# Two diffusion-backbone layers on one core: the order of the three token tiles in attention

## The reference

```python
for l in range(2):
    # prompt: attends to the prompt alone
    a_q, a_k, a_v, b_q, b_k, b_v = project_heads(xp * (1 + p_sc1) + p_sh1, w_in[l], qk_gain[l])
    mix_p = mixer_output(...)                    # 128 keys
    # sample: attends to its 256 keys and 128 cached ones
    a_q, ... = project_heads(xs * (1 + s_sc1) + s_sh1, w_in[l], qk_gain[l])   # and axial rotary
    a_k = concatenate([a_k, cache_a_k[:, l]], axis=1)                         # likewise a_v, b_k, b_v
    mix_s = mixer_output(...)                    # 384 keys
    # mixer_output: 4 differential heads, softmax(q1 k1) - lam * softmax(q2 k2), times v, RMS-normed,
    #               8 GQA query heads over 2 kv heads, both concatenated and times w_out[l]
    # then x = LayerNorm(alpha * x + gate * mix), a dense SwiGLU (layer 0) or top-2-of-8 experts (layer 1)
```

## Time and profile before

| | us |
|---|---|
| median of 3 runs | 1724.61 (1721.42 to 1729.32) |
| the profiled execution, its own time | 1731.87 |
| span of its profile | 1730.0 |
| attention of layer 0: first scores to the transposes of o | 142.77 to 235.66 |
| attention of layer 1, the same | 681.37 to 774.51 |

### The profile page before, as it was taken

The page is one execution under the profiler, slowest core; times in us unless marked ns, Lnnn a source line. Parts: engine busy times, 40 slices in busy tenths (PEclk is TensorE's granted clock), DMA queues, the critical chain, the costliest instruction groups (busy, mean ns, idle before and its releaser), DMA issues. The chain is left out here.

```text
span 1730.0 us, 24774 instructions
## 1 busy us (share of the span) xinstructions
PE 1554.8 (90%) x9179; PEld 1036.2 (60%) x9180; DVE 752.9 (44%) x1215; ACT 575.3 (33%) x979; POOL 90.6 (5%) x109
## 2 busy tenths in 40 slices
PE   4798989999999899988898999989999799999891
PEld 1684577788887486466623565645556477677430
DVE  0473776333333654675501443434344443233215
ACT  0433545223331442450202333433343433233101
POOL 2010012200000010000100000000000000000002
PEclk8899999999999899999699999999999999999896
DMA  9244536933441644532999999999999378787992
GB/s 344 98 146 161 195 122 208 342 122 113 146 146 50 219 138 137 192 133 74 401 364 376 385 389 393 386 343 378 375 393 376 126 292 292 276 294 264 359 352 101
DMA packets 206705, 432.49 MB, mean 250 GB/s; under 512 B 11896, under 2 KB 52856, under 8 KB 206304
## 3 DMA queue, kind: packets, MB, share of 16 engines
q1 hardware_dynamic: 195712, 390.64, 62.3%
q0 software_dynamic: 7712, 29.05, 4.6%
q10 hardware_dynamic: 3136, 10.88, 1.9%
HBM read 409.55 MB, written 20.97 MB: 249 GB/s over the span
## 5 line engine op out<-in xcount | busy, mean ns | idle before, releaser
L2004 PE MATMUL ps<-d_ring_parts,scratch_parts 128*128 128x512 f32 (+1 forms) x444 | 172.1, 388 | 13.9 <-DVE hT_parts L1318 9.1
L1825 DVE TENSOR_TENSOR cst<-cst,ps 128x256 f32<-128x256 f32 (+2 forms) x89 | 32.7, 368 | 241.5 <-ACT cst L1156 241.5
L2405 PE MATMUL ps<-ring,hT 128*32 128x256 f32 x1760 | 119.9, 389 | 10.3 <-DMA ring<-in_w_moe_up 9.2
L2004 PE MATMUL ps<-gu_ring_parts,scratch_parts 128*128 128x512 f32 (+1 forms) x336 | 128.7, 383 | 0.0
L2399 PE MATMUL ps<-ring,hT 128*64 128x512 f32 (+1 forms) x512 | 113.1, 584 | 15.9 <-issue 8.5
L2004 PE MATMUL ps<-d_ring_parts,hT_parts 128*128 128x512 f32 (+1 forms) x312 | 119.0, 382 | 0.0
L1181 ACT ACTIVATE qkv_parts<-ring 128x1024 fp32r<-128x1024 f32 x102 | 103.1, 1050 | 13.2 <-issue 13.0
L2004 PEld LDWEIGHTS ps<-d_ring_parts,scratch_parts 128*128 128x128 f32 x444 | 84.7, 191 | 32.2 <-issue 9.3
L2004 PE MATMUL ps<-gu_ring_parts,o_parts 128*128 128x512 f32 x264 | 104.0, 394 | 0.0
L2405 PEld LDWEIGHTS ps<-ring,hT 128*32 128x32 f32 x1760 | 55.9, 111 | 61.2 <-issue 15.7
L1164 ACT ACTIVATE cst<-ps 128x128 f32<-128x128 f32 (+1 forms) x51 | 16.0, 315 | 224.9 <-PE ps L2421 215.5
(11 more groups left out here) (385 smaller groups left out, 3150.1 us busy)
## 6 DMA issues: line engine op xcount, KB each, us to landing
ring<-in_w_moe_gate SPq DMA_DIRECT2D x176, 512.0 KB, 9.7
ring<-in_w_moe_up SPq DMA_DIRECT2D x176, 512.0 KB, 11.1
ring<-in_w_moe_down SPq DMA_DIRECT2D x176, 512.0 KB, 9.6
gu_ring<-in_w_ada SPq DMA_DIRECT2D x48, 1024.0 KB, 7.4
gu_ring<-in_w_in SPq DMA_DIRECT2D x16, 1024.0 KB, 7.4
gu_ring<-in_w_ffn_gate SPq DMA_DIRECT2D x11, 1024.0 KB, 5.5
gu_ring<-in_w_ffn_up SPq DMA_DIRECT2D x11, 1024.0 KB, 8.1
d_ring<-in_w_ffn_down SPq DMA_DIRECT2D x11, 1024.0 KB, 10.9
```

Of the source, the lines that this page charges most:

```text
L1825: dve.tensor_tensor(hid_e[0:rows, k % 2, 0:f], hid_e[0:rows, k % 2, 0:f], ps[0:rows, 6 + k % 2, f:2 * f], ALU.mult).then_inc(hid_ready, 1 ...
L2004: ins = pe.matmul(out, a, w, start=(start and n == 0), stop=(stop and n == 2))
L2405: ins = pe.matmul(ps[32 * j:32 * j + 32, bank, 0:FC].rearrange("p (a f) -> p a f", a=2), hT[:, kc, col:col + 32], wt[:, :, P * j:P * j + P ...
```

## The change

Units 0 to 7 become tile 1, units 8 to 15 tile 2, and units 16 to 23 tile 0; within a tile the pairs keep their order. `norm_part`, which had the tile from the unit's number, follows the same table.

```diff
+TILE_ORDER = [1, 2, 0]
+
+
 def tile_of_unit(v):
-    return v // 8, v % 8
+    return TILE_ORDER[v // 8], v % 8
...
             def norm_part(l, v):
 
-                i, step = divmod(v - 3, 8)
+                place, step = divmod(v - 3, 8)
                 if v < 3 or step > 3:
                     return
+                i = TILE_ORDER[place]
```

## The result

| | before | the change |
|---|---|---|
| median of the runs, us | 1724.3 (13 runs, 1718.66 to 1731.41) | 1732.39 (13 runs, 1726.37 to 1737.63) |
| ratio, 95% interval | | 1.0042 [1.0026, 1.0058] |
| profiled execution, span, us | 1731.87, 1730.0 | 1728.16, 1726.3 |
| TensorE, VectorE busy, us | 1554.8, 752.9 | 1545.0, 753.7 |

The change costs 0.42%, 7.2 us by the ratio (the two medians lie 8.1 us apart). A second measurement of the same kernel beside other runs of the kernel before gave 1731.24 us and 1.0034 [1.0019, 1.0049], 5.9 us. The profiled execution of the changed kernel happens to be one of its fastest and is even shorter than that of before. So totals of single profiles say nothing here.

What follows compares the result with a forecast made beforehand. TensorE's work bounds the attention ahead of T, VectorE's list behind it. Per layer 7.3 + 0.6 + 0.5 - 3.2 = +5.2 us, +10.4 for two, from the median 1724.61 to 1735.0 us; range 1726.0 to 1743.0.

Steps and rivals of the forecast that it cites:

- (a): TensorE's scores, turns and weighings ahead of T: sample units replace prompt units there, +7.3 us a layer, counted in full.
- T: The moment when adaLN piece 10 is done, 216.55 us in layer 0 before; forecast 8 us later after the first scores.
- Rival 2: TensorE has slack in the sample's units, only 58% real load: (a) shrinks to 4.2, 1728.8 us; chance 0.11.
- (b): TensorE's waits ahead of T for exponentials, P^T copies, probability tiles and adaLN rows: +0.6 us a layer.
- (c): Clock in the head: both slow stretches at 1.2 GHz stay, +0.5 us a layer for the chance of a third.
- Rival 1: The head keeps 2.4 GHz, both slow stretches go: +1.4 us a layer, 1727.4 us; chance 0.15.
- T later by less than 5 us: Sign that the forecast is wrong, pointing to rivals 1 and 2: look at the clock, then at the unit steps.
- (d): Behind T, up to the first projection matmul: shorter prompt units end it at T + 22.4 instead of T + 25.6, -3.2 us.
- 2 us of cover: Behind T: VectorE's list has 2 us to spare over ScalarE's wait for w_out's second piece, costed at nothing.

Runs made afterwards that it cites:

- the middle order: Tile order 1, 0, 2 instead of the change's 1, 2, 0, so the prompt's units stand in the middle: 1727.75 us, 1.0012 of before.
- the late pair: All four w_out splits and rests put behind the attention loop, in both orders: prompt first 1740.09 us (1.0086 of before), prompt last 1734.90 us (1.0052).
- the last order: The change's order, prompt last, with w_out's first piece fetched earlier, two splits at 18 and 19, rests at 19 and 22: 1725.57 us, 1.0007 of before.
- the filled kernel: The kernel before, order 0, 1, 2, plus three unused 384-column matmuls in TensorE's waits in the head: 1724.32 us, 0.9996 of before.
- the late kernel: The change's order, prompt last, with all four w_out splits and rests behind the attention loop: 1734.90 us, 1.0052 of before.
- the last pair: Two w_out halves split at 18 and 19, rests at 19 and 22, in both orders: prompt first 1725.40 us (0.9998 of before), prompt last 1725.57 us (1.0007).
- the orders with equal work: The kernel before (order 0, 1, 2) and the one with tile order 1, 0, 2, which has equal work ahead of T: 1727.75 us, 1.0012 of before.
- prompt first: The kernel before, order 0, 1, 2, with one w_out rest (half 10) made by GpSimd instead of VectorE: 1732.18 us, 1.0043 of before.
- prompt last: The change, order 1, 2, 0, with one w_out rest (half 10) made by GpSimd instead of VectorE: 1735.70 us, 1.0058 of before.

## Why the prediction was right, and what was mis-sized

The forecast was 1735.0 us; it came out 2.6 us lower, slower as forecast and in the range given, though 0.8 us under the 1733.2 at which the prediction let "slower" begin. By its terms, per layer:

- **(a), work ahead of T: +7.3 forecast, +6.4 measured** as TensorE's busy time of the change less that of the middle order at almost equal clock. The method holds, start-to-start times of each step by their counts; it was 0.9 us too high, of which up to half a microsecond may be the place of the slow stretch. Rival 2, that only 58% of TensorE's busy time is load, would have been 4.2 and falls. The Trainium skill (Trainium Kernel Development and Optimization, Performance Expectations) puts weight-load busy time above matmul busy time for judging how close a kernel is to roofline. Taken as a price for moved work, as in rival 2, it does not agree with this trace.
- **(b), waits ahead of T: +0.6 forecast, 0.0 measured**: TensorE idle 6.95 us before, 6.92 after. Line by line: the exponential's wait +0.5 (1.4 to 1.9), as worked out; the P^T waits +0.4 (1.7 to 2.1; forecast 0.6); the row waits -0.6 (0.8 to 0.2; forecast 0.5); the combined probability tile 2.6 to 2.5.
- **(c), the clock: +0.5 forecast, -1.1 measured.** This is the step whose mechanism failed. I argued that the slow stretches follow the two waits, that the waits do not shrink, and that both stretches stay. The waits even grew, and both stretches went; one other came. Rival 1 had the direction, and two thirds of its 3.3 us did not come: the number went from two to one, and going from 6.8 to 3.4 us at 1.2 GHz gave 1.1. A stretch does cost up to what I put: 1.7 us in the head, 1.2 at 214 us.
- Sum ahead of T: 6.4 + 0.0 - 1.1 = 5.3, against the measured 5.2 and 5.0, and the forecast 8.4. "T later by less than 5 us" was my sign for being wrong, so this came out at its very edge, and rival 1, which that sign names, did come in part.
- **(d), behind T: -3.2 forecast, -2.7 and -2.8 measured.** The schedule came out step by step: the 1.0 us wait of VectorE for unit 22's exponentials is 0.98, the first rest at T + 5.97 (forecast 6.0), the transposes at T + 16.1 (15.9), the projection at T + 22.9 (22.4). The last 0.3 us are the transposes themselves, 5.38 instead of 4.96 us: behind longer waits the granted clock is 0.59 from their start to the projection, before it was 0.66. The w_out transfer cost ScalarE 0.55 us and nobody else, as its 2 us of cover said.

Two layers give +4.7 us in the profiles where I summed +10.4, while the runs show +7.2 and +5.9. So the total owes part of its closeness to luck: the attention gave less than half of the sum, and 1 to 2.5 us came from outside the stretch that I had priced. These I could not place: from the projection of layer 0 to the first scores of layer 1, the same instructions in each, the profiled execution of before needs 681.37 - 242.19 = 439.2 us, that of the change 677.30 - 243.37 = 433.9 and its repetition 436.8, so one profile of each kernel can't show it. In all twelve comparisons the runs show more time over before than the profiled attentions do, 0.8 to 3.4 us and in the late pair 8.0 and 6.6. They share one profile of before, whose 1731.87 us is longer than every one of its 13 runs above, so that profile may be the untypical side; this is not shown. That the attention's loss is work moved ahead of T, of which VectorE's list behind T hides the return, is shown by the middle order (the change's head, no loss that the runs can tell, a tail of 19.11 us) and by the late pair (with the list away the tail gives back 6.8 us instead of 3.0). What decides whether a slow stretch comes stays open.

## What to carry to other kernels

Short work is worth its time only where its own engine sets the end. Before reordering units of different size, find for each stretch which engine's list ends last, price the moved steps start to start there, and ask what hides them at their new place. If the tail is bound by side work of another engine, as the w_out rests here, moving that side work can be worth as much as moving the units (here the last order's tail lost 2.8 us by it); but put it by the order of that engine's instructions, never by its busy share: two rests of 2.3 us at indices 18 and 20 cost 4.7 and 5.1 us, at 19 and 22 a wait of 0.6 or 0.7.

## What the runs showed of the hardware

- The granted clock fell to 0.61 over 214 to 218 us, where TensorE's busy time is 4.00 of 4.00 us, among scores and turns of 128 columns and half an adaLN piece, and it stayed at 1.00 in a head with waits of 1.9 and 2.0 us. Neither the length of a wait nor busy time told me where it would fall. In two executions of the same instructions it fell once in the head and once at 214 us, and in the filled kernel once at 177 us in one layer and twice, at 682 and 713 us, in the other.
- Time at 1.2 GHz costs at most half of itself: a stretch of 3.4 us cost 1.7 us between the layers of the late kernel, 1.6 between those of the filled one, 1.6 and 1.5 between those of the last pair, 1.2 where it lay at 214 us and 1.1 between the orders with equal work.
- A GpSimd subtract of 2048 elements a partition took 4.5 us where VectorE needs 2.29, and held a VectorE instruction of 0.69 us for 3.08 us (prompt first) and 4.34 us (prompt last). The kernel before shows the other direction, unseen by me: GpSimd's small reciprocal root takes 1.01 us in those kernels and 2.98 beside VectorE's first rest (225.24 to 227.53 us):

```profile
225.41 2.98 POOL L776 TENSOR_TENSOR rstd<-var_in,neg_half 128x4 f32<-128x4 f32 x1 [27.75 <-DVE var_in L1458]
```
